# GpSimd makes the sums of weight blocks of the feed-forward's seven products, in place of VectorE

## The reference

```python
hx2 = modulate(rms_norm(x, g_ffn_pre[l]), sh2, sc2)
x = x + gt2 * rms_norm(conv_ffn(hx2, w_up[l], conv_ffn_w[l], conv_ffn_b[l], w_down[l]), g_ffn_post[l])

def conv_ffn(h, w_up, conv_w, conv_b, w_down):
    up = depthwise_conv(h @ w_up, conv_w, conv_b, FFN_CONV // 2)   # 2048 -> 2 x 5632
    g, v = jnp.split(up, 2, axis=-1)
    return (jax.nn.gelu(g, approximate=True) * v) @ w_down         # 5632 -> 2048
```

## Time and profile before

| what | value |
| --- | --- |
| median of three runs | 2042.01 us (2041.34 to 2043.75) |
| profiled execution | 2046.65 us |
| its span, first to last instruction | 2044.8 us |
| mean granted TensorE clock | 0.993 of full |
| TensorE matmuls busy | 2002.4 us, 98% |
| VectorE busy | 1617.5 us, 79% |
| ScalarE busy | 965.3 us, 47% |
| GpSimd busy | 276.8 us, 14% |
| mean transfer rate | 176 GB/s |

### The profile page before, as it was taken

How to read it: one execution, slowest core, us unless ns; L and a number is a source line. 1 busy time by engine, 2 the same in 40 slices (tenths; PEclk the granted TensorE clock), 3 DMA queues, 4 the chain that set the end, 5 groups by cost and what they waited for, 6 DMA issues and landing times.

```text
span 2044.8 us, 32425 instructions
## 1 busy us (share of the span) xinstructions
PE 2002.4 (98%) x13122; PEld 1778.5 (87%) x13122; DVE 1617.5 (79%) x2461; ACT 965.3 (47%) x1332; POOL 276.8 (14%) x317
## 2 busy tenths in 40 slices
PE   7999999999999999999999999999999999999989
PEld 3678887888777788999999999999999999999878
DVE  5566979877888997888787788778878778877677
ACT  5346676552422355444444444544444444444443
POOL 0000001001111001112211211211221121111202
PEclk9999999999999999999999999999999999999999
DMA  9953325433987435566656656656665665665673
GB/s 394 408 219 126 131 93 180 139 115 99 340 300 269 164 124 181 124 171 165 155 149 172 165 145 160 169 139 162 166 155 148 172 165 145 159 141 137 145 253 115
DMA packets 130646, 360.74 MB, mean 176 GB/s; under 512 B 12288, under 2 KB 56320, under 8 KB 127936
## 3 DMA queue, kind: packets, MB, share of 16 engines
q1 hardware_dynamic: 68544, 247.28, 34.4%
q0 software_dynamic: 61136, 110.60, 25.0%
q10 hardware_dynamic: 816, 0.79, 0.1%
HBM read 305.14 MB, written 53.48 MB: 175 GB/s over the span
## 4 chain that ended last, share of the span: by engine, by line
PE 71%; issue 7%; DVE 2%; ACT 2%; POOL 1%; DMA 1%; SPq 0%; POOLq 0%; ACTq 0%; DVEq 0%
PE bank L1103 23%; PE bank L1105 23%; PE bank L1104 23%; POOL down_summed_d L651 1%; DMA x<-in_stream 1%; PE bank L1214 0%; DMA down_summed_d<-acc 0%; DVE acc L2308 0%; PE bank L1399 0%; PE bank L1423 0%; ACT sums_hi L682 0%; ACT w_hi L680 0%; PE bank L1309 0%; DVE w_lo L1654 0%; DVE sums_lo L1652 0%
## 5 line engine op out<-in xcount | busy, mean ns | idle before, releaser
L1103 PE MATMUL bank<-h_hi,w_hi 128*128 128x256 f32 (+1 forms) x1728 | 569.2, 329 | 10.4 <-ACT acc L1016 4.6
L1104 PE MATMUL bank<-h_lo,w_hi 128*128 128x256 f32 (+1 forms) x1728 | 565.7, 327 | 0.0
L1105 PE MATMUL bank<-h_hi,w_lo 128*128 128x256 f32 (+1 forms) x1728 | 565.5, 327 | 0.0
L1103 PEld LDWEIGHTS bank<-h_hi,w_hi 128*128 128x128 f32 x1728 | 325.6, 188 | 45.2 <-issue 12.5
L1105 PEld LDWEIGHTS bank<-h_hi,w_lo 128*128 128x128 f32 x1728 | 325.3, 188 | 30.6
L1104 PEld LDWEIGHTS bank<-h_lo,w_hi 128*128 128x128 f32 x1728 | 325.7, 188 | 24.2
L651 POOL DMA_DIRECT2D down_summed_d<-acc x156 | 184.8, 1191 | 938.4 <-ACT acc L1016 927.9
L680 ACT ACTIVATE w_hi<-w_raw 128x1024 fp32r<-128x1024 f32 x160 | 169.4, 1059 | 236.7 <-DVE w_raw L2178 236.7
L1103 PE MATMUL bank<-act_hi,w_hi 128*128 128x512 f32 (+1 forms) x688 | 266.0, 387 | 8.2 <-DVE acc L2280 6.3
L1104 PE MATMUL bank<-act_lo,w_hi 128*128 128x512 f32 (+1 forms) x688 | 265.2, 386 | 0.0
L1105 PE MATMUL bank<-act_hi,w_lo 128*128 128x512 f32 (+1 forms) x688 | 265.2, 386 | 0.0
(11 more groups left out here) (345 smaller groups left out, 3850.2 us busy)
## 6 DMA issues: line engine op xcount, KB each, us to landing
w_raw<-in_stream SPq DMA_DIRECT2D x339, 512.0 KB, 4.0
ada_raw<-in_adabg POOLq DMA_DIRECT2D x112, 512.0 KB, 5.7
down_summed_d<-acc POOLq DMA_DIRECT2D x172, 256.0 KB, 4.9
ada_raw<-in_ada SPq DMA_DIRECT2D x64, 512.0 KB, 13.8
x<-in_x_t SPq DMA_DIRECT2D x4, 1024.0 KB, 8.3
acc<-in_adabg SPq DMA_DIRECT2D x8, 512.0 KB, 6.1
x<-in_x_t POOLq DMA_DIRECT2D x4, 1024.0 KB, 9.3
x_kept_d<-x SPq DMA_DIRECT2D x4, 1024.0 KB, 5.6
```

Of the source, the lines that this page charges most:

```text
L1103: t.matmul(out, w, v, start=start, stop=False)
L1104: t.matmul(out, w, v_l, start=False, stop=False)
L1105: return t.matmul(out, w_l, v, start=False, stop=stop)
```

## The change

`sum_blocks` moves from VectorE's list to GpSimd's. It waits for the unit's load and for the free set of sum buffers as before, does the same four operations on GpSimd, with waits on a semaphore of GpSimd's own between those that depend on each other, and then gives `blocks_summed`, for which ScalarE waits. In GpSimd's list the sums stand between transfers. After the transfers of pair 3's tiles 0 to 2, 3 to 5 and 6 to 8 come the sums of pair 4's first three units. For each later pair the sums of the fourth unit and of the units three, four and more further on come first, as far as these are up units of the next pair; then, within the tiles of each down unit, the transfers of the first half, the sum of the unit three later, and the transfers of the other half. Nothing else is changed; ScalarE's, TensorE's and SP's lists stay.

```diff
+            def sum_blocks(n):
+                pool.wait_ge(*raw_sem(n))
+                raw = raw_unit(n)
+                r1, r2, r3, r4 = (raw[:, 2 * P * i:2 * P * i + 2 * P] for i in range(4))
+                sums, _, _ = sums_of(n)
+                s1, s2, s3 = (sums[:, 2 * P * i:2 * P * i + 2 * P] for i in range(3))
+                if WSUM[n] >= SETS:
+                    pool.wait_ge(*used(max(u for u in WSUM if WSUM[u] == WSUM[n] - SETS)))
+                chain.step(g.tensor_tensor(s1, r3, r4, ALU.add))
+                chain.step(g.tensor_tensor(s3, r1, r3, ALU.subtract))
+                chain.wait()
+                chain.step(g.tensor_tensor(s2, s1, r1, ALU.subtract))
+                chain.wait()
+                g.tensor_tensor(r3, r2, s2, ALU.subtract).then_inc(blocks_summed, 1)
...
-            for n in range(FIRST, FT):
-                for m, blocks in DOWN[n]:
-                    add_down(taken, m, blocks[0][0] == 0)
-                    taken += 1
+            def sums_if(n):
+                if n in WSUM:
+                    sum_blocks(n)
+
+            for t, (m, blocks) in enumerate(DOWN[FIRST]):
+                if t in (3, 6, 9):
+                    sum_blocks(UP[CH] + (t - 3) // 3)
+                add_down(t, m, True)
+            taken = TILES_BY[FIRST]
+            for n in range(CH, FT):
+                for unit in range(UP[n] + 3, UP[n] + 7):
+                    sums_if(unit)
+                for unit in DOWN_UNITS[n]:
+                    for t in TILES_IN[unit]:
+                        if t == TILES_IN[unit][len(TILES_IN[unit]) // 2]:
+                            sums_if(unit + 3)
+                        m, blocks = DOWN[n][t - TILES_BY[n - 1]]
+                        add_down(t, m, blocks[0][0] == 0)
...
-                sum_blocks(u + 3)
                 convolve_gate(n - 1)
                 lo(u + 3)
-                sums_if(u + 4)
                 convolve_value(n - 1)
...
                 for unit in d:
-                    sums_if(unit + 3)
                     lo(unit + 2)
```

More of the change, by code:

```diff
@@ L429, in build @@
         ada_eaten, ada_summed, ada_read = sem("ada_eaten"), sem("ada_summed"), sem("ada_read")
-        act_chain, dve_chain = sem("act_chain"), sem("dve_chain")
+        act_chain, dve_chain, pool_chain = sem("act_chain"), sem("dve_chain"), sem("pool_chain")
         csig_done, csil_done, exp_lam, decay_done = sem("csig_done"), sem("csil_done"), sem("exp_lam"), sem("decay_done")
@@ L606, in _ @@
         def _(pool):
+            chain = Chain(pool, pool_chain)
+            g = nc.gpsimd
             def load_ada(first, stop):
@@ L2161, in multiply @@
                 v.tensor_tensor(cg[:, n % 2, :], cg[:, n % 2, :], cv[:, :], ALU.mult).then_inc(ffn_prod, 1)
[L2163 to L2178, removed]
             def common_sums(n):
@@ L2198, in pair_sums @@
                 v.tensor_tensor(up_sum[:, L:L + H], up_sum[:, L:L + H], alone_v[:, 0:H], ALU.add).then_inc(sum_v, 1)
-            def sums_if(n):
-                if n in WSUM:
-                    sum_blocks(n)
             u, d = UP[FIRST], DOWN_UNITS[FIRST][0]
@@ L2230, in _ @@
             lo(d + 3)
-            sum_blocks(UP[CH])
             lo(d + 4)
-            sum_blocks(UP[CH] + 1)
             lo(UP[CH])
-            sum_blocks(UP[CH] + 2)
             lo(UP[CH] + 1)
@@ L2244, in _ @@
                     pair_sums(n - 1)
-                sum_blocks(u + 3)
                 convolve_gate(n - 1)
                 lo(u + 3)
-                sums_if(u + 4)
                 convolve_value(n - 1)
                 lo(u + 4)
-                sums_if(u + 5)
                 multiply(n - 1)
@@ L2254, in _ @@
                 split_act(n - 1, (n - 1) % CH)
-                sums_if(u + 6)
                 for unit in d:
```

## The result

| what | before | after |
| --- | --- | --- |
| median | 2042.88 us (2041.34 to 2043.76, 4 runs) | 2351.81 us (2348.20 to 2354.61, 4 runs) |
| span of the profiled execution | 2044.8 us | 2351.2 us |
| mean granted TensorE clock | 0.993 | 0.937 |

The ratio is 1.151, with a 95% interval of 1.149 to 1.153: 309 us slower. The forecast was 2338 us, in a range of 2140 to 2440.

The account below looks back on a forecast made before the run. TensorE, busy 98% of the span, was taken as the bound. Wait 216, contention 16 and clock 64 make 296 us: 2046.65 profiled becomes 2343, the median 4.6 lower, 2338 us; range 2140 to 2440.

Parts of the forecast that it names:

- The wait, 5.4 us x 40 = 216: By a walk from down tile 0, TensorE waits 5.4 us for tile 3's bank at forty boundaries, 216 us.
- The boundaries of another form: After pairs 5 and 42 about 3.5 us, pair 6 7 us, pairs 3 and 41 6 to 8; near 5.4 each.
- VectorE's work, 0: In the feed-forward stage, 271 us of sums leave VectorE, worth 0 because TensorE's full windows cover them.
- A sum, 3.1 us: Four operations on GpSimd take 3.1 us per unit, between 1.67 and 4.8, priced from its addition at the kernel's end.
- Contention, 0.4 us a boundary: GpSimd's sums meeting VectorE's operations cost 0.4 us a boundary, between 0 and 3.4: 16 us.
- Rival C: GpSimd's additions meet VectorE's at every turn, sums take 4.8 us, 3.4 us a boundary: 2458 us; chance 0.07.
- The fourth unit's deadline, 0 us: The sum of a pair's fourth unit, 1.4 us longer, leaves 2.2 of 3.6 us to spare: 0 us.
- Clock, 1.6 us a boundary = 64: After each gap TensorE works some 3.5 us at half clock and loses 1.6 us: 64 us over the boundaries.
- rival B: The same wait at the boundaries, but TensorE's clock holds: 2274 us; chance 0.16.
- Load of code, 0: Two MODIFY_POOL_CONFIG records of 0.5 us move to GpSimd's first sum, near 770 us: 0, at most 1 us.
- Rival E: Each GpSimd change from transfer to addition loads code again, 1 us or more, twice: 2418 us at least; chance 0.05.
- Rival D: A GpSimd sum starts beside a transfer's issue, so the wait is 1.8 us and the kernel 2130 us; chance 0.08.

Follow-up runs that it names:

- e1: Changed kernel, in GpSimd's queue each pair's first held-up sum ahead of down tile 0's transfer, the second right behind it: 2070.09 us, ratio 1.014.
- e5: Kernel before, with only the sum behind down tile 0's transfer in each pair on GpSimd, the others on VectorE: 2052.48 us, ratio 1.004.
- e6: Changed kernel with one GpSimd addition 768 wide per sum in place of four of 256, so sums differ: 2227.78 us, ratio 1.091.
- e8: Kernel before, with the sums of pairs 8 to 39 on GpSimd, in its queue ahead of the waiting transfers: 2048.59 us, ratio 1.003.
- e2: Changed kernel, but ScalarE drains all tiles of a down unit before it rounds, instead of half: 2186.81 us, ratio 1.070.
- e4: Changed kernel with 42 unused matmuls a pair ahead of TensorE's wait for tile 3's bank: 2298.19 us, ratio 1.126.
- e3: Kernel before, with only the sum behind down tile 2's transfer in each pair on GpSimd, the others on VectorE: 2193.77 us, ratio 1.073.

## Why the prediction was right

**The wait, 5.4 us x 40 = 216.** Right in place, cause and nearly in size. The steps of the walk stand in the trace. Counted from the drain of tile 0 (1400.68 in rows 5, 1523.38 here, 122.70 later), the walk has transfer 0 at 1524.44, the end of sum A at 1528.7, drain 1 at 1530.5, the end of sum B at 1537.1, drain 3 at 1538.8 and TensorE at 1539.5. The trace has 1524.33, 1528.61, 1530.41, 1536.91, 1538.70 and 1539.33. The wait is 5.1 us in the steady part; all waits on drains, with the one at the start, grew by 206 us. (That one has no releaser in the list, but it ends at 790.36, where the first of pair 3's last three drains, begun at 789.68, is over.) e1 and e5 show that order and not price makes it, e6 that each us of a sum counts twice.

**The boundaries of another form.** Near 5.4 each was right as a sum and rough one by one: 7.6 us after pair 3 (6 to 8 in the prediction), 3.5 after pair 4 (5.4), 4.3 after pair 5 (4.6), 1.3 and 5.4 after pair 6 (7), 0.9 and 9.0 after pair 41 (6 to 8), 6.0 after pair 42 (4.0).

**VectorE's work, 0.** Right, though its busy time fell by 159 us and not by the 271 that the prediction named as a sign, mostly because what it kept became longer beside GpSimd's additions. e5 and e8, in which GpSimd takes a part of it without a new wait in the steady part, are not faster than before.

**A sum, 3.1 us.** Right: 3.09 and 3.04 in the loop, with the row of the tail as its only source. Over all 160 the last operation has 737 ns in the median:

```profile
L670 POOL TENSOR_TENSOR w_raw<-w_raw,sums_raw x160: 722/737/1606, 771.0 to 2264.6; 128x256 f32<-128x256 f32 x160
```

**Contention, 0.4 us a boundary.** Too large in the loop and too small outside it. In the loop the sums met next to nothing: the `ada_acc` operation (1523.45 to 1524.73) was over before sum A began, and the 74 sums behind a transfer take 3.04 us in the median, 3.95 at most. Outside it one sum of a pair meets VectorE's low halves and takes 5.2 to 5.8 us (from 900 to 1900 us VectorE's L1687 has a mean of 1700 ns, where the same subtraction had 1218), and it cost no wait of TensorE, because it stands where there is time. The sum of such a case in the middle of the stage:

```profile
1286.06 0.95 POOL L665 TENSOR_TENSOR sums_raw<-w_raw 128x256 f32<-128x256 f32 x1 [5.10 <-DMA w_raw<-in_stream]
1286.98 1.71 POOL L666 TENSOR_TENSOR sums_raw<-w_raw 128x256 f32<-128x256 f32 x1
...
1289.93 1.60 POOL L670 TENSOR_TENSOR w_raw<-w_raw,sums_raw 128x256 f32<-128x256 f32 x1
```

The Trainium skill, "SBUF — State Buffer", "Who interferes with whom", has a VectorE instruction with two SBUF inputs contend with a GpSimd one that reads SBUF, by an exclusive lock. The traces agree that they contend, and e2's subtraction of 0.95 us that took 3.15 was held for longer than one addition of 0.74. Rival C (2458 us, sums of 4.8 us in the loop) is refuted: the order of the work kept VectorE away from the two sums that count, as the prediction argued. (The prediction's 7.8 us for a sum that waits out four subtractions should read 3.1 + 4 x 1.22 = 8.0; nothing rests on it.)

**The fourth unit's deadline, 0 us.** Right for this kernel, since the loop bound first, and the margin was misjudged all the same: the walk let that sum start when the buffers come free, while in e2 it starts behind transfer 3 and the load, runs in contention and is rounded behind two other operations, and TensorE comes 2.00 us late to the unit. It was the next bound behind the one predicted.

**Clock, 1.6 us a boundary = 64.** The fall came at each boundary, so rival B (2274 us) is refuted. The size was too small: TensorE worked at half clock from 1539.33 to 1544.1, 4.7 us and not 3.5, and lost 2.3 where the prediction had 1.6. What is not in the listed waits is 100 us, against 64; e4 got back some 50 of them. The prediction's sum came out within 10 us of the 306 partly by luck: this term was 36 us low, and the wait and the contention together (232 against 206) 26 us high.

**Load of code, 0.** Right. The two records stand at 768.6, of 33 and 37 ns and not 507, and the first addition starts at 768.72:

```profile
L665 POOLq MODIFY_POOL_CONFIG  x2: 33/35/37, 768.6 to 768.7; - x2
```

The first sum after them takes 3.06 us like the others. The 6 us that "GPSIMD Engine Reference", "Instruction dispatch", in the Trainium skill gives for a first call are not seen here; an earlier moment, if there was one, the trace does not show. Rival E is refuted by the same view: there are two such records in all, both ahead of the first addition, and none at a later change. Rival D is refuted by GpSimd's timeline, where the first addition ends at 1526.29, 0.77 us after the issue's end at 1525.52, though its record begins before that: it ran behind the issue, not beside it.

## What to carry to other kernels

Before work moves to an engine that seems idle, write down what its queue waits for just ahead of the new place and who waits for the work. If the two are the same engine, neither can run ahead, and each us of the moved work is paid once for every turn of that loop. The same instructions ahead of the waiting transfers cost next to nothing in the steady part here (2.9 us in 33 periods, 30.0 us a period against 37.5). Opening such a loop on one side only shows the next deadline, so walk that one too, with the queue's other entries in it. And where TensorE was full, freeing VectorE gave nothing (e8).

## What was not expected of the hardware

TensorE's granted clock fell to one half after 29 of 34 gaps of 2.25 us, one in each 34 us (e3). Matmuls put into a gap for nothing made the kernel 54 us faster (e4). An operation of VectorE with two SBUF operands went from 0.95 to 3.15 us beside GpSimd's additions, and GpSimd's of 128x256 from 0.73 to 1.7 us beside VectorE's. The records of the load of code were 507 ns long in one place and 35 ns in another.
